# A three-block expert table and gathers for the fourth block: where the products, the gather ticks and two loads stand

## What is computed

```
    q = jnp.einsum('bsd,de->bse', h, w_q)...reshape(B, S, PEER_HEADS, PEER_D_KEY)
    v1, i1 = lax.top_k(s1, PEER_TOPK)
    v2, i2 = lax.top_k(s2, PEER_TOPK)
    cand = (v1[..., :, None] + v2[..., None, :]).reshape(B, S, PEER_HEADS, PEER_TOPK * PEER_TOPK)
    vals, c = lax.top_k(cand, PEER_TOPK)
    expert = e1 * PEER_N_KEYS + e2
    gate = jax.nn.softmax(vals, axis=-1)
    def block(args):
        u = u_tab[eb]
        act = jax.nn.gelu(jnp.einsum('td,ted->te', hb, u), approximate=False)
        v = v_tab[eb]
        return jnp.einsum('te,ted->td', gb * act, v)
```

## Time and profile before

| | us |
|---|---|
| median of 3 runs (3005.68 to 3009.01) | 3006.16 |
| the profiled execution | 3007.56 |
| its span | 3005.8 |
| TensorE busy | 2787.5 (93%) |
| VectorE busy | 1972.8 (66%) |
| ScalarE busy | 1140.9 (38%) |
| GpSimd busy | 543.3 (18%) |

### The profile page before, as it was taken

One profiled execution on the slowest core, in us unless ns is written; L12 is line 12 of the kernel. 1 busy time (PEld: TensorE's weight loads), 2 busy tenths in 40 slices (PEclk: granted clock), 3 DMA queues, 4 the chain that ended last, 5 costly groups with the idle time before them and its releaser, 6 DMA issues.

```text
span 3005.8 us, 36696 instructions
## 1 busy us (share of the span) xinstructions
PE 2787.5 (93%) x14045; PEld 2364.5 (79%) x14045; DVE 1972.8 (66%) x3643; ACT 1140.9 (38%) x1678; POOL 543.3 (18%) x390
## 2 busy tenths in 40 slices
PE   8999999999998998988997999999997987899997
PEld 6787878887777888887996888888886556688876
DVE  3335665665555789899995887887886485444434
ACT  5445144223224333336884222222223444322222
POOL 0111221120002767663111111111110011000000
PEclk9999999999999999998998999999998999999999
DMA  4112100005552666576888788888882200222220
GB/s 155 50 50 98 57 29 29 29 29 196 210 203 86 227 243 249 215 265 238 323 311 319 283 302 308 292 292 293 292 291 86 79 29 2 98 92 98 96 98 28
DMA packets 141358, 501.17 MB, mean 167 GB/s; under 512 B 13401, under 2 KB 67073, under 8 KB 111617
## 3 DMA queue, kind: packets, MB, share of 16 engines
q1 hardware_dynamic: 122752, 364.60, 34.5%
q0 software_dynamic: 18432, 134.23, 11.3%
HBM read 450.53 MB, written 48.25 MB: 166 GB/s over the span
## 4 chain that ended last, share of the span: by engine, by line
PE 62%; DVE 23%; DMA 7%; ACT 4%; issue 3%; POOL 1%; SPq 0%; DVEq 0%; ACTq 0%; POOLq 0%
PE bank L244 16%; PE bank L245 16%; PE bank L246 16%; DMA gs<-in_uv_dram,idx 4%; DVE HA L2058 3%; DVE bank L1713 2%; DVE gs L1700 2%; DVE xn L1508 1%; PE bank L2658 1%; PE bank L1090 1%; PE bank L1080 1%; PE bank L713 1%; PE bank L1096 1%; DMA w_raw<-in_w_in_dram 1%; DVE uhl L1635 1%
## 5 line engine op out<-in xcount | busy, mean ns | idle before, releaser
L244 PE MATMUL bank<-HH,uhl 128*128 128x384 f32 x1024 | 358.3, 350 | 45.3 <-POOL uhl L1635 41.4
L245 PE MATMUL bank<-HL,uhl 128*128 128x384 f32 x1024 | 352.7, 344 | 0.0
L246 PE MATMUL bank<-HH,uhl 128*128 128x384 f32 x1024 | 352.3, 344 | 0.0
L244 PE MATMUL bank<-vhl,awhl 128*128 128x512 f32 x768 | 300.4, 391 | 6.8 <-DVE awhl L2291 6.8
L246 PE MATMUL bank<-vhl,awhl 128*128 128x512 f32 x768 | 300.3, 391 | 0.0
L245 PE MATMUL bank<-vhl,awhl 128*128 128x512 f32 x768 | 300.3, 391 | 0.0
L1689 POOL DMA_INDIRECT gs<-in_uv_dram,idx x128 | 161.2, 1259 | 753.6 <-DVE x L1713 497.0
L2242 ACT ACTIVATE vhl<-vraw 128x1024 fp32r<-128x1024 f32 x128 | 135.8, 1061 | 419.2 <-PE bank L246 253.4
L244 PEld LDWEIGHTS bank<-HH,uhl 128*128 128x128 f32 x1024 | 198.8, 194 | 52.6 <-issue 36.5
L1635 POOL TENSOR_TENSOR uhl<-ur,uhl 128x1024 fp32r<-128x1024 f32 x66 | 159.0, 2418 | 421.2 <-ACT uhl L1629 420.8
L2247 DVE TENSOR_TENSOR vhl<-vraw,vhl 128x1024 fp32r<-128x1024 f32 x128 | 156.5, 1223 | 104.0 <-ACT vhl L2242 103.9
(11 more groups left out here) (420 smaller groups left out, 6233.6 us busy)
## 6 DMA issues: line engine op xcount, KB each, us to landing
ur<-in_peer_u_dram SPq DMA_DIRECT2D x128, 512.0 KB, 5.9
vraw<-in_peer_v_dram SPq DMA_DIRECT2D x128, 512.0 KB, 4.5
w_raw<-in_w_in_dram SPq DMA_DIRECT2D x36, 1024.0 KB, 4.9
xn<-in_ada_rows_dram SPq DMA_DIRECT2D x48, 512.0 KB, 4.7
g_scratch<-stg SPq DMA_DIRECT2D x12, 2048.0 KB, 11.0
gti<-g_scratch SPq DMA_DIRECT2D x16, 1536.0 KB, 10.0
wf_raw<-in_f_w_in_dram SPq DMA_DIRECT2D x22, 1024.0 KB, 4.8
act_scratch<-ag SPq DMA_DIRECT2D x96, 192.0 KB, 4.2
```

Of the source, the lines that this page charges most:

```text
L244: e.matmul(out, l[0], r[0], start=start, stop=False)
L245: e.matmul(out, l[0], r[1], start=False, stop=False)
L246: return e.matmul(out, l[1], r[0], start=False, stop=stop)
```

## The change

Three up products (chunks 64 to 66) move from the gate stage to the end of the search stage, ahead of the transposes, with their Gelus, stores and loads; GpSimd makes low halves 66 to 68. In the gate stage the other 24 products stand at every fourth group instead of every third (27 before). Of the twelve ticks four stay in the gate stage (groups 5, 28, 51, 74); eight go to the experts' stage, where 39 ticks instead of 31 are spread at 3.2 columns apart. v chunks 0 and 1 are split two products later by ScalarE, and the second load of gates stands behind v chunk 4 in the experts' stage instead of ahead of v chunk 2.

```diff
--- before.py
+++ after.py
@@ -1609,7 +1609,7 @@
 
-    D2 = 64
+    D2 = 67
 
     def u_low(n):
         return UP[3] if n < D2 + 2 else UP[2]
@@ -1678,7 +1678,7 @@
     dot = new.sb("dot", [P, P])
     ga = new.sb("ga", [P, P])
     h2p, sump = (bank[:, i:i + 2, :].rearrange("p a b -> p (a b)") for i in (4, 6))
-    T3 = 33
+    T3 = 25
 
     def pool_gather(e, t):
         if t < NB:
@@ -1816,6 +1816,8 @@
                 pe_scores(e, c + 1)
             for n in range(4, 8):
                 pe_up(e, R5, 8 * c + n)
+        for n in range(64, D2):
+            pe_up(e, R5, n)
         e.wait_ge(*V.of("e", 7))
         for tb in range(3):
             b = R5.take("eT", tb)
@@ -1878,6 +1880,8 @@
                 act_tick(e, 3 * c - 1)
             act_up(e, R5, 8 * c + 6)
             act_up(e, R5, 8 * c + 7)
+        for n in range(64, D2):
+            act_up(e, R5, n)
         for tb in range(3):
             e.wait_ge(*T.of("eT", tb))
             e.activation(eT[:, :, blk(tb)], R5.bank("eT", tb)[:, 0:3 * P].rearrange("p (a c) -> p a c", a=3),
@@ -1990,6 +1994,8 @@
                 pool_gather(e, 0)
                 pool_gather(e, 1)
             lo(9)
+        for n in range(66, D2 + 2):
+            u_lo(e, n)
 
     def sp_route(e):
         all_done(e, *MG)
@@ -2012,6 +2018,8 @@
                     fetch(e, W2, 2 * c + 5)
                 if n == 5 and c + 2 < 8:
                     sp_keys(e, c + 2)
+        for n in range(64, D2):
+            sp_up(e, n)
 
     def sp_keys(e, c):
         if c >= 2:
@@ -2037,9 +2045,9 @@
     ph0.close()
     iota = const("iota")
     io4 = iota.unsqueeze(1).broadcast_to([P, 4, P])
-    up_at = {q: D2 + q // 3 for q in range(2, 81, 3)}
+    up_at = {4 * i + 2: D2 + i for i in range(24)}
     up_end = range(D2 + len(up_at), NE)
-    tick_at = {q: 21 + q // 8 for q in range(5, NQ, 8)}
+    tick_at = {5 + 23 * i: 21 + i for i in range(T3 - 21)}
 
@@ -2109,7 +2117,7 @@
                 act_tick(e, tick_at[q])
         for n in up_end:
             act_up(e, R6, n)
-            if n == NE - 4:
+            if n == NE - 2:
                 all_done(e, *GT)
                 act_v(e, 0)
                 act_v(e, 1)
@@ -2124,6 +2132,7 @@
                 dve_tick(e, tick_at[q])
             if q - 4 in up_at:
                 u_lo(e, up_at[q - 4] + 2)
+        u_lo(e, up_end[0] + 1)
         for n in up_end:
             if n == NE - 2:
                 dve_sums(e, T3 - 1)
@@ -2159,7 +2168,6 @@
         sp_gti(e, 0)
         for n in up_end[1:]:
             sp_up(e, n)
-        sp_gti(e, 1)
 
@@ -2177,6 +2185,7 @@
         whl = [new.sb(f"awhl{i}", [P, 2, DT], F32R) for i in range(3)]
         agd = [new.sb(f"agd{i}", [P, DT]) for i in range(3)]
     new.scope = exps
+    tick_in = {1 + 16 * i // 5: T3 + i for i in range(NB - T3)}
     xs5 = [ur[:, i, :] for i in range(3)] + [vraw[:, 0, :]]
     tmps5 = [vraw[:, 1, 0:512], vraw[:, 1, 512:1024]]
     sums = lambda tb, dh: banks[2 * tb + dh]
@@ -2254,8 +2263,8 @@
         for j in range(P):
             if j >= 2:
                 act_v(e, j)
-            if j % 4 == 2:
-                act_tick(e, T3 + j // 4)
+            if j - 1 in tick_in:
+                act_tick(e, tick_in[j - 1])
             if place[j] >= NE:
                 act_up(e, R7, place[j])
         e.wait_ge(*GA[2].of("ax", NB - 1))
@@ -2289,10 +2298,10 @@
             e.tensor_copy(wh, agd[j % 3][:, :]).then_inc(*V.up("wh", j))
             e.wait_ge(*V.of("wh", j))
             e.tensor_tensor(wl, agd[j % 3][:, :], r32(wh), ALU.subtract).then_inc(*V.up("w", j))
-            if j % 4 == 1 and T3 + j // 4 < NB:
-                dve_dots(e, T3 + j // 4)
-            if j % 4 == 3 and T3 + j // 4 < NB:
-                dve_sums(e, T3 + j // 4)
+            if j in tick_in:
+                dve_dots(e, tick_in[j])
+            if j - 2 in tick_in:
+                dve_sums(e, tick_in[j - 2])
         var_x(e, A, V, 3, 1)
         scale_x(e, A, V, xs5, 3, 1)
         split_lo(e, WI, 0)
@@ -2319,7 +2328,7 @@
             if place[j] >= NE:
                 sp_up(e, place[j])
             sp_act(e, j + 3)
-            if j % 8 == 2 and 8 <= j < P - 8:
+            if j % 8 == 2 and j < P - 8:
                 sp_gti(e, j // 8 + 1)
 
```

## The result

The changed kernel takes 2995.73 us, the median of 20 runs (2988.53 to 3004.32), against 3005.80 (2999.06 to 3010.6) for the kernel before on the same chips. The ratio is **0.9969, 95% interval 0.9960 to 0.9978: 9.3 us faster**. The forecast was 20.8 us faster: the sign was right and the size was not.

What follows compares the result with a forecast made beforehand. VectorE was taken to bound the gate stage, TensorE the experts' stage. Gates -32.1, search end +16.3, joint -5, experts 0 sum to -20.8 us: 2985.4 against the 3006.16 median; forecast's own range 2978 to 2996, 8-in-10 range 2973 to 3001.

Steps and rivals of the forecast that it cites:

- Gate stage: Gate stage proper: with VectorE relieved, ScalarE longest at 187.4 us; stage falls from 229.6 to 197.5, a gain of 32.1.
- the 6 us for ticks: Gate stage: each of four ticks stops VectorE and ends a product 1 to 2 us late, 6 us in all.
- Rival (a): Gate stage: ScalarE's 19.4 us of waits for products remain, stage 216.9 us, whole 3005; chance 0.11.
- End of the search: Search end: three products ahead of the transposes, 14.6 us with a cold start, delay VectorE's gate start by 16.3 us.
- Experts' stage: Experts' stage: eight more ticks, 40 us of VectorE, stay covered by TensorE; cost 0, bounds -2 and +6.
- Rival (b): Experts' stage: DMA becomes the bound, 16.8 MB more cost 51 us, whole 3036; chance 0.06.
- Joint: Between gates and experts: moved gates' load lets v chunk 2 land sooner, 5 us gained, bounds 0 and 8.
- The part that the forecast counted as free: Joint: two high halves of u go ahead of those of v 0 and 1 on ScalarE; no cost counted.
- The forecast's remark on products and gates: Search end and gate stage: moving 12.6 us of TensorE work costs 16.3, saves 12.8 of TensorE and 3.4 of VectorE.

Runs made afterwards that it cites:

- the cured kernels: Two variants of the changed kernel: experts' stage dots and sums over 256 of 1024 columns (0.9945), or gate loads from the third on cut to one of twelve tiles (0.9957).
- short ticks: Changed kernel with dots and sums of the experts' stage over 256 of 1024 columns, gathers unchanged; ratio 0.9945, 16.5 us faster than the kernel before.
- the transposes first: Changed kernel with the route transposes and ScalarE's copies of them put back ahead of products 64 to 66; ratio 0.9970 to the kernel before.
- the kernel with the earlier halves: Changed kernel plus gate loads in halves, u chunk 97 first, transposes first, tick 20's Gelu later, low halves 65, 66 and ScalarE's first one-hots earlier; ratio 0.9907.

## Why the prediction was right or wrong

**Gate stage, right.** Forecast 197.5, measured 197.8. VectorE's sum of 182.0 stands against 182.92 busy us, ScalarE's 187.4 against 185.81, TensorE's 185.2 against 188.34. It was TensorE and not ScalarE that came out longest. The stage is TensorE's 188.34 us, 2.6 ahead of its first gate matmul, and five waits for VectorE's HA of 6.8 us together, which stand behind the four ticks: the 6 us for ticks were of the right size. Rival (a), ScalarE's waits for products, did not come true. They fell from 19.4 us to 8.6, first row of the waits in the gate stage:

```profile
ACT ag L1659 <- PE bank L246: 8.6, 9, 2.2
PE bank L2093 <- DVE HA L2066: 6.8, 5, 2.3
```

**End of the search, right.** 15.6 against 16.3. Product 64 waited 4.87 us and started cold (the granted clock was 0.50 from 1373.88 to 1377.29), GpSimd's last low half ended at 1388.91 ahead of VectorE's start, and the three products took 14.1 us against 14.6.

**Experts' stage, wrong: this is the step that failed.** The forecast had it at 0, between -2 and +6, and it was +10.3 (12.0 above the 645.9 of the cured kernels; 8.4 of them stand in the trace as gaps of TensorE). It set 13.4 us of VectorE work against 15.1 of TensorE and a DMA share of 0.88 against 1, each by itself, and found both covered. Both figures were about right, VectorE busy 539.17 of 646.50 us at a share of 0.83. What failed is the conclusion: the two covers are not independent. The load that VectorE's lateness delays is the load whose landing makes VectorE late. Rival (b) named a point from which it decides, a load and split of a v chunk taking longer than two columns (10 us), and then judged it by the mean share. Neither measure decides. The longest load alone was 10.9 us before and 13.1 with short ticks, both without a gap, and 12.5 in the changed kernel with ten. What the runs show is that VectorE's added work and late landings stop TensorE together, and that taking away either is enough.

**Joint, half of it.** The mechanism of the moved gates' load is as forecast, the third product 4.9 us sooner when it is moved alone, but most of that is lost again in the stage behind it. In the changed kernel 2.7 were left. The part that the forecast counted as free, two high halves of u ahead of those of v, costs 2.2. That it does so because it releases loads that compete with u chunk 97 was argued from the order of the issues and not shown.

**The whole.** -20.8 became -8.6 in the trace and -9.3 timed. Most of what was lost was lost in the stage that took over the eight ticks. That 2995.73 lies within the stated range is luck as far as this term goes: +10.3 is beyond its own bound of +6, and the rest of the range made room for it. The forecast's remark on products and gates, a move that costs 16.3 and saves 12.8 of TensorE, was borne out: 15.6 us against 13.5 in the gate stage. The three products earn nothing that could be measured, and the ticks alone would have done the same.

## What to carry to other kernels

Work that is moved under a bound engine is free only if the loops through it have slack at their worst moment. Follow each buffer's loop once round, with the longest landing time of the row in place of the median, and with the engine's in-order queue in it. Where such a loop has no slack and a large transfer of low urgency shares the queues with small urgent ones, split it and spread it: here the same bytes cost the stage 12 us in one piece and nothing in two. Where the loop had slack, the split gained nothing. And an engine that stands idle behind a wait may cost nothing at all: ask what the engine at the end of the chain was doing in that time.

## What the runs showed of the hardware

The time to landing of a 0.5 MB load went from 3.4 to 12.5 us at a mean DMA share of 0.84, and its longest value fell by 2.7 us when a neighbour of 1.5 MB was cut in two, at a share of 0.87. With short ticks, at the same share of 0.87 and with that neighbour whole, it was 13.1. So the mean share tells little of what one load will take. VectorE's 2.51 us for one instruction beside a GpSimd subtraction has no counterpart in the changed kernel, whose longest HA takes 0.48 us: there the last low half of GpSimd (1386.51, 2.40 us) ended ahead of VectorE's first one. Where VectorE starts sooner, it meets them again. With the transposes first, four HA took 5.68 us beside two low halves of GpSimd, in the kernel with the earlier halves 6.08 (section 6), against 1.11 for four alone. By the Trainium skill (SBUF — State Buffer, Who interferes with whom), which has the two engines hold a shared pair of ports for a whole instruction in turn, this is what is to be expected; the traces agree. It made 2.2 us of VectorE's time in the kernel before and 5.0 in one group of the kernel with the earlier halves, where TensorE waited 1.26 us for it.
